# Three page buffers instead of two for the paged FoX sample attention of a two-layer hybrid decoder step

## The reference

```python
k_past = cache_fox_k[l, page_table].reshape(DB, past_len, FOX_H, HEAD_DIM)
v_past = cache_fox_v[l, page_table].reshape(DB, past_len, FOX_H, HEAD_DIM)
...
s_past = jnp.einsum('bthd,bshd->bhts', q, k_past) * scale + (cn[..., :, None] - cp[..., None, :])
s_new = jnp.einsum('bthd,bshd->bhts', q, k) * scale + (cn[..., :, None] - cn[..., None, :])
p = jax.nn.softmax(jnp.concatenate([s_past, s_new], -1), axis=-1)
out = einsum('bhts,bshd->bthd', p[..., :P], v_past) + einsum('bhts,bshd->bthd', p[..., P:], v)
```

## Time and profile before

| | |
|---|---|
| median of 3 runs | 4450.54 us (4433.85 to 4451.39) |
| profiled execution | 4439.32 us, span 4437.8 us |
| PE busy | 4107.8 us, 93% of the span |
| DVE, ACT, POOL busy | 31%, 15%, 7% |
| mean granted TensorE clock | 0.951 |
| DMA | 249.98 MB, mean 56 GB/s |

### The profile page before, as it was taken

One profiled execution on the slowest core, in us unless ns is written; L12 is line 12 of the kernel. 1 busy time (PEld: TensorE's weight loads), 2 busy tenths in 40 slices (PEclk: granted clock), 3 DMA queues, 4 the chain that ended last, 5 costly groups with the idle time before them and its releaser, 6 DMA issues.

```text
span 4437.8 us, 58111 instructions
## 1 busy us (share of the span) xinstructions
PE 4107.8 (93%) x21754; PEld 3067.6 (69%) x21754; DVE 1383.9 (31%) x2997; ACT 664.5 (15%) x1307; POOL 294.6 (7%) x518
## 2 busy tenths in 40 slices
PE   8888999988799999999997889999878899999998
PEld 5677668765457888866656776777545588888665
DVE  3344322334224333300043442233442333332000
ACT  2222101243100000000022221013431000000000
POOL 1000000220200000000010000003111000000000
PEclk9998999999899999999998899999988899999998
DMA  4300020121821111121123001101236111112112
GB/s 125 25 0 0 15 58 25 51 66 58 286 76 29 47 38 45 44 79 39 34 77 10 0 0 36 47 20 47 97 116 221 50 38 47 38 47 84 39 33 64
DMA packets 277954, 249.98 MB, mean 56 GB/s; under 512 B 24636, under 2 KB 237696, under 8 KB 276496
## 3 DMA queue, kind: packets, MB, share of 16 engines
q1 hardware_dynamic: 244400, 144.89, 13.1%
q0 software_dynamic: 33376, 102.70, 7.0%
HBM read 214.70 MB, written 32.83 MB: 56 GB/s over the span
## 4 chain that ended last, share of the span: by engine, by line
PE 82%; DVE 7%; issue 6%; POOLq 2%; POOL 1%; ACT 1%; DMA 1%; DVEq 0%; ACTq 0%; SPq 0%
PE ps L849 78%; PE ps L853 4%; POOL big L749 1%; POOLq L748 1%; POOLq L749 1%; DVE hT L2285 0%; DVE hT L1668 0%; DVE big L1890 0%; ACT wd L2629 0%; DMA ring<-in_w_out 0%; DVE big L1898 0%; DMA big<-in_cache_fox_k 0%; DVE big L1860 0%; DVE big L1853 0%; DVE big L1851 0%
## 5 line engine op out<-in xcount | busy, mean ns | idle before, releaser
L849 PE MATMUL ps<-hT,ring 128*128 128x352 f32 (+1 forms) x3712 | 1073.7, 440 | 23.6 <-DMA ring<-in_w_out 13.2
L849 PEld LDWEIGHTS ps<-hT,ring 128*128 128x128 f32 x3712 | 712.7, 194 | 331.4 <-issue 26.4
L849 PE MATMUL ps<-big,wd 128*128 128x352 f32 (+3 forms) x2576 | 700.2, 431 | 9.7 <-DVE big L1860 7.2
L849 PEld LDWEIGHTS ps<-big,wd 128*128 128x128 f32 (+2 forms) x2576 | 455.1, 189 | 250.5 <-issue 16.1
L849 PE MATMUL ps<-xT,ring 128*128 128x264 f32 x1408 | 345.9, 389 | 13.4 <-DVE xT L2313 13.4
L849 PEld LDWEIGHTS ps<-xT,ring 128*128 128x128 f32 x1408 | 269.5, 192 | 60.7 <-DVE xT L2313 14.2
L849 PEld LDWEIGHTS ps<-ring,hT 128*128 128x128 f32 (+1 forms) x2304 | 259.9, 183 | 16.1 <-issue 13.5
L849 PE MATMUL ps<-ring,hT 128*128 128x128 f32 (+1 forms) x2304 | 265.1, 275 | 2.6 <-ACT xT L2508 2.6
L849 PE MATMUL ps<-hT,wd 128*128 128x264 f32 x1056 | 258.4, 388 | 0.0
L849 PE MATMUL ps<-big 128*128 128x128 f32 (+5 forms) x1492 | 219.0, 308 | 23.6 <-DVE big L1862 7.7
L849 PEld LDWEIGHTS ps<-hT,wd 128*128 128x128 f32 x1056 | 202.2, 191 | 35.2
(11 more groups left out here) (376 smaller groups left out, 3843.3 us busy)
## 6 DMA issues: line engine op xcount, KB each, us to landing
ring<-in_w_in SPq DMA_DIRECT2D x60, 512.0 KB, 3.8
ring<-in_w_gate SPq DMA_DIRECT2D x44, 512.0 KB, 4.1
ring<-in_w_up SPq DMA_DIRECT2D x44, 512.0 KB, 4.1
wd<-in_w_down SPq DMA_DIRECT2D x16, 1408.0 KB, 7.0
x_kept<-xT POOLq DMA_DIRECT2D x32, 528.0 KB, 3.9
xT<-x_kept POOLq DMA_DIRECT2D x32, 528.0 KB, 9.2
big<-in_cache_fox_k SPq DMA_DIRECT2D x64, 256.0 KB, 5.2
big<-in_cache_fox_k POOLq DMA_DIRECT2D x64, 256.0 KB, 5.4
```

The source lines that it names most:

```text
L849: return pe.matmul(out, lhsT, rhs, start=start, stop=stop, skip_group_check=True)
```

## The change

Halves are numbered n = 0 to 7 in the order in which they are used: keys, keys, values, values of group 0, then of group 1. Half n goes into buffer n modulo 3. The third buffer is `fqk` (`xT`): sequence b's pages lie in tiles b and 4 + b, which pair b of the prompt has finished with. So half 2, the first values of group 0, is loaded during the prompt, four pages after each pair. Half 3 waits for `T33`, half 4 for `T73`, half 5 for `V0`, half 6 for `V1` (all of group 0), half 7 for `T33` of group 1. The turned keys of odd units move from the ring to tiles 6 and 7 of `hT`, and `smn` (4 numbers) to the end of tile 4. Behind half 7 SP issues three `w_out` blocks at once, and the fourth, in the slot of `vn`, after `V0` of group 1. POOL waits for `T73` of group 1 before it fetches x back into `xT`. PE's loop over the two groups is written out; those of DVE and ACT stay.

```diff
-        page_at = lambda a, b, j: pages[a][:, b, FW * j:FW * j + FW]
+        def page_at(n, b, j):
+            if n % 3 == 2:
+                return fqk[:, 4 * (j // 2) + b, FW * (j % 2):FW * (j % 2) + FW]
+            return pages[n % 3][:, b, FW * j:FW * j + FW]
...
-        keyt = [region((sil, 0), 4, HPG * PG), region((ringf, 0), 4, HPG * PG)]
+        keys0 = region((sil, 0), 4, HPG * PG)
+        keyt = lambda u, b: hT[:, 6 + b // 2, 512 * (b % 2):512 * (b % 2) + 512] if u % 2 else keys0[:, b, :]
...
-        smn = hT[:, 5, 0:TS]
+        smn = hT[:, 4, NP:NP + TS]
```

On SP:

```diff
-                half("cache_fox_k", key_in, 0, 0, range(1))
+                half(0, range(1))
+                half(2, range(1))
                 sp.wait_ge(fp_dve, FP_DVE.at(l, "1o"))
...
-                half("cache_fox_k", key_in, 0, 1, range(2))
+                half(1, range(2))
+                half(2, range(1, 2))
+                sp.wait_ge(fp_dve, FP_DVE.at(l, "2o"))
+                sp.sem_inc(passed, 1)
+                half(2, range(2, 3))
                 sp.wait_ge(fp_dve, FP_DVE.at(l, "3o"))
...
+                half(1, range(2, 4))
+                half(2, range(3, 4))
+                for n_, it, done in ((3, 2 * l, "T33"), (4, 2 * l, "T73"), (5, 2 * l, "V0"), (6, 2 * l, "V1"), (7, 2 * l + 1, "T33")):
+                    sp.wait_ge(fgr_pe, G_PE.at(it, done))
+                    sp.sem_inc(passed, 1)
+                    half(n_, range(4))
-                sp.wait_ge(fgr_pe, G_PE.at(l * 2 + 1, "F"))
                 for j in range(J_OUT, J_OUT + RING):
+                    if j == J_OUT + RING - 1:
+                        sp.wait_ge(fgr_pe, G_PE.at(l * 2 + 1, "V0"))
                     sp.sem_inc(passed, 1)
                     free(l, j)
                     load(l, j, w_block(l, I["w_out"], P * (j - J_OUT)))
```

On POOL the halves move in the same way (with the odd pages), the third buffer's pages among the prompt's pairs, and x waits:

```diff
+                    if p < 3:
+                        half(2, range(p, p + 1))
...
+                pool.wait_ge(fgr_pe, G_PE.at(2 * l + 1, "T73"))
                 pool.wait_ge(x_out, l * (32 * KT) + 16 * KT)
```

On PE:

```diff
-                with pe.Fori(0, 2) as g:
+                for g in range(2):
...
-                                last = tr(ps[:, 3 + b, P * j:P * j + P], page_at(a, b, j)[:, P * p:P * p + P])
+                                last = tr(ps[:, 3 + b, P * j:P * j + P], page_at(4 * g + a, b, j)[:, P * p:P * p + P])
...
-                                last = mm(ps[o, 7, :], pts[:, HPG * a + j, o], page_at(a, b, j), False, a == 1 and j == HPG - 1)
+                                last = mm(ps[o, 7, :], pts[:, HPG * a + j, o], page_at(4 * g + 2 + a, b, j), False, a == 1 and j == HPG - 1)
```

More of the change, by code:

```diff
@@ L558, in _, with half @@
                 sp.sem_inc(passed, 1)
-                def half(kind, done, g, a, seqs):
+                def half(n_, seqs):
+                    g, a, keys = n_ // 4, n_ % 2, n_ % 4 < 2
+                    kind, done = ("cache_fox_k", key_in) if keys else ("cache_fox_v", value_in)
                     for b in seqs:
@@ L563, in half @@
                             n = sp.value_load(ptab[0:1, bass.ds(g * (4 * NPG) + (b * NPG + a * HPG + j), 1)], min_val=0, max_val=N_POOL - 1)
-                            sp.dma_start(page_at(a, b, j), I[kind][bass.ds(l, 1), bass.ds(n, 1)].rearrange("a n p h d -> p (a n h d)")).then_inc(done[a][0], 16)
-                half("cache_fox_k", key_in, 0, 0, range(1, 4))
+                            sp.dma_start(page_at(n_, b, j), I[kind][bass.ds(l, 1), bass.ds(n, 1)].rearrange("a n p h d -> p (a n h d)")).then_inc(done[a][0], 16)
+                half(0, range(1, 4))
                 sp.wait_ge(fp_dve, FP_DVE.at(l, "0o"))
                 sp.sem_inc(passed, 1)
-                half("cache_fox_k", key_in, 0, 0, range(1))
+                half(0, range(1))
+                half(2, range(1))
                 sp.wait_ge(fp_dve, FP_DVE.at(l, "1o"))
@@ L769, in half @@
                             n = pool.value_load(ptab[0:1, bass.ds(g * (4 * NPG) + (b * NPG + a * HPG + j), 1)], min_val=0, max_val=N_POOL - 1)
-                            pool.dma_start(page_at(a, b, j), I[kind][bass.ds(l, 1), bass.ds(n, 1)].rearrange("a n p h d -> p (a n h d)")).then_inc(done[a][1], 16)
+                            pool.dma_start(page_at(n_, b, j), I[kind][bass.ds(l, 1), bass.ds(n, 1)].rearrange("a n p h d -> p (a n h d)")).then_inc(done[a][1], 16)
                 pool.wait_ge(fg_act, FG_ACT.at(l, "kos"))
@@ L798, in _ @@
                 pool.sem_inc(passed, 1)
[L799 to L810, removed]
+                half(1, range(2, 4))
+                half(2, range(3, 4))
+                for n_, it, done in ((3, 2 * l, "T33"), (4, 2 * l, "T73"), (5, 2 * l, "V0"), (6, 2 * l, "V1"), (7, 2 * l + 1, "T33")):
+                    pool.wait_ge(fgr_pe, G_PE.at(it, done))
+                    pool.sem_inc(passed, 1)
+                    half(n_, range(4))
+                pool.wait_ge(fgr_pe, G_PE.at(2 * l + 1, "T73"))
                 pool.wait_ge(x_out, l * (32 * KT) + 16 * KT)
@@ L1533, in key_scores @@
                         for b in range(4):
-                            last = mm(ps[NS * b:NS * b + NS, a, :], cur_q[:, b, p, :], keyt[u % 2][:, b, :], False, p == 3)
+                            last = mm(ps[NS * b:NS * b + NS, a, :], cur_q[:, b, p, :], keyt(u, b), False, p == 3)
                         G_PE.mark(last, fgr_pe, f"S{u}")
@@ L2220, in _ @@
                             on(gp(f"T{u}{b}"))
-                            gm(v.tensor_copy(keyt[u % 2][:, b, :], ps[:, 3 + b, :]), f"kt{u}{b}")
+                            gm(v.tensor_copy(keyt(u, b), ps[:, 3 + b, :]), f"kt{u}{b}")
                     on(gp(f"S{UNITS[-1]}"))
@@ L2661, in _ @@
                             on(gp(f"T{u}{b}"))
-                            gm(a.copy(keyt[u % 2][:, b, :], ps[:, 3 + b, :]), f"kt{u}{b}")
+                            gm(a.copy(keyt(u, b), ps[:, 3 + b, :]), f"kt{u}{b}")
                     on(gd("neg"))
```

## The result

| | before | after |
|---|---|---|
| median | 4435.33 us of 5 runs (4427.22 to 4451.39) | 4401.91 us of 5 runs (4395.92 to 4406.84) |
| profiled execution, span | 4437.8 us | 4400.2 us |
| mean granted TensorE clock | 0.951 | 0.954 |

The ratio is 0.9916, 95% interval 0.9898 to 0.9933: faster by more than 0.5%. The sign and the mechanism were as forecast; the time, 4401.9, lies 22 us under the 4423.7 and 2 us under the low end of the range. The medians stand 33.4 us apart where the sum said 26.9.

A forecast was written before the change was run, and what follows sets the result against it. PE, 82% of the chain, bounds the kernel; only its transfer waits can go. 11.2 + 12.5 + 0.9 + 0.9 + 1.7 − 0.3 = 26.9 us off the median 4450.5 gives 4423.7 us, range 4404 to 4438.

The forecast's parts named there:

- The sign and the mechanism: Whole kernel: faster, chance 0.68, because PE's waits for keys, values and `w_out` beside the sample attention go.
- the base: Starting time from which the gain was subtracted: the median of the runs, 4450.5 us.
- the clock's two terms: Faster clock once waits go: 0.9 us in group 1's first transposes, 1.7 us in the first eight output matmuls.
- the keys: Sample attention, group 1: half 4 lands early, so PE's key waits of 6.54 and 4.67 us go, 11.2 us.
- the weights: Start of the output jobs: `w_out` issued behind half 7 is hidden, saving 6.29 + 6.17 = 12.5 us.
- the values: Sample attention, group 0 of layer 1: the wait for the second value half goes, 0.9 us.
- What is late next: Half 5, keys of group 1 in the third buffer: there by 1151.4, needed at 1156.9, margin 5.5 us.
- rival 2: Group 1, unit 4: the wait moves to half 5; chance 0.12, or 0.03 for slower than before, such as 4457 us.
- The prompt: Prompt pairs: half 2's loads stretch a store at pair 1's head, costing 0.3 us in all, 1.4 at most.
- Rivals 3 and 4: 3: `w_out` lands no earlier, 4437.8 us, chance 0.10. 4: prompt pays some 15 us at pair heads, 4438, chance 0.05.
- Rival 1: Group 1's transposes and the first output matmuls both run at the high clock: 31.8 us less, 4418.7 us, chance 0.10.

The follow-up runs named there:

- 1: The kernel before, unchanged, run again against itself (the repeated kernel before): 4436.73 us, ratio 1.0002.
- 5: The kernel before with only PE's loop over the two groups written out: 4437.28 us, ratio 0.9995.
- 7: The kernel before with POOL's eight RWKV shift-state stores per layer moved behind its copies for chunk 1: 4437.53 us, ratio 0.9995.
- weights alone (3): The kernel before, two page buffers kept, with turned keys in `hT` and three `w_out` blocks issued behind the last value half: 4430.5 us, ratio 0.9982.
- pages alone (4): The change with the wait for `F` put back ahead of the `w_out` blocks: 4418.16 us, ratio 0.9952.
- 2: The change, unedited, run again against the kernel before (the repeated change): 4405.39 us, ratio 0.9923.
- 6: The change with POOL's eight RWKV shift-state stores per layer moved behind its copies for chunk 1: 4407.08 us, ratio 0.9928.
- 8: The change with POOL's eight RWKV shift-state stores per layer moved behind its copies for chunk 4: 4402.31 us, ratio 0.9924.
- 9: The change without the seven stores per layer of the samples' RWKV shift state: 4393.5 us, ratio 0.9908.

## Why the prediction was right and wrong

The stage of the sample attention, both layers together, in all eleven profiles, each worked out as above, and how much of it PE was busy:

| kernel | stage, us | PE busy in it, us |
|---|---|---|
| before (four: as read, 1, 5, 7) | 249.1, 251.9, 252.5, 251.9 | 181.4, 185.1, 184.2, 183.4 |
| weights alone (3) | 244.4 | 181.8 |
| pages alone (4) | 231.4 | 179.9 |
| the change (five: as read, 2, 6, 8, 9) | 219.9, 219.9, 220.6, 218.0, 220.8 | 176.0, 176.0, 177.1, 174.2, 177.1 |

The windows of the pair as read (columns as in the earlier trace rows), before and after:

```profile
1082.55:1206.46 123.91, 89.64 (x643) 51.48 (x643) 40.29 (x79) 25.30 (x44) 32.62 (x60) 0.78 0.78 273
3268.79:3393.96 125.17, 91.73 (x643) 51.97 (x644) 40.29 (x79) 25.30 (x44) 32.64 (x60) 0.80 0.77 270
```
```profile
1079.54:1190.05 110.51, 88.47 (x643) 50.42 (x643) 40.45 (x79) 25.30 (x44) 28.91 (x54) 0.83 0.78 278
3245.18:3354.54 109.36, 87.51 (x643) 49.69 (x644) 40.45 (x79) 25.30 (x44) 28.90 (x54) 0.83 0.79 281
```

The means of the first and the last line, 251.3 and 219.8, are **31.5 us** apart, and the medians of experiments 1 and 2 stand 31.3 apart. So no part of the gain has to be sought outside this stage. Of the 31.5, PE's idle time gives 24.0 and its busy time 7.4 (rounded): the same number of matmuls runs in less time, at a granted clock of 0.83 over the stage after 0.78 and 0.80.

**What failed, in short.** The forecast of 4423.7 missed by 21.8 us. Of these 13.8 are the base, a median of three runs; 4.4 are the gain, 31.3 instead of 26.9, where the clock's two terms, 0.9 + 1.7 = 2.6, were mis-sized and the runs show 7.4; the last 3.5 are the five runs of the result, whose median lies below that of the six of experiment 2.

**Right:** *the keys, the weights, the values.* All three waits are gone; of `w_out` 0.62 us a layer remain where 0.38 was left over by the sum. The 24.0 us of idle time answer to the 24.6 of these three terms. *What is late next:* nothing; half 5 was in time, and rival 2 fell in both layers, also in its slower form. *The prompt:* pairs 1 to 3, from the end of pair 0 to that of pair 3, took 138.93 us before and 140.68 after in layer 0, 137.99 and 136.27 in layer 1: no cost that shows, where −0.3 was taken. By the Trainium skill, "DMA: Bandwidth & Descriptors", section "Issuing engines are not separate DMA queues", 1.4 us would have been lost; these rows, −1.75 and +1.72, show no such loss in the sum of the two layers. But the same stretch of layer 0 took 142.27 in the repeated kernel before, 3.3 us more than in the first, so a loss of this size could hide. Rivals 3 and 4 fell too.

**Wrong, the base:** "from the median the time is **4423.7**". The three runs had their median at 4450.5; 24 runs beside experiments 1 and 2 gave 4436.7, so 13.8 us of the miss are in the start and none of them in the change. Single runs follow the granted clock of the whole execution: of the 24, the two at 0.946 took 4449.1 and 4456.0 us, the one at 0.955 took 4423.5. The profiled execution at hand, 4439.3, was nearer, and the sum against it, 4412.4, would have been 7 us off the 4405.4 of the repeated change. The low end, 4404, was set between the two places that the fastest of three runs gave; it had to hold a low base and a larger gain together.

**Wrong, the clock:** "I take the middle, **1.7**" for the first output matmuls. They took 4.05 + 4.49 before and 2.60 + 2.60 after, a gain of 3.3, near the upper end of 3.5; over all profiles their mean fell from 9.1 to 5.2. The windows of the change (PE, PEld, DVE, ACT, POOL busy, granted clock, DMA share, GB/s) show the two places where I set rows against each other:

```profile
1137.80:1140.50 2.70, 2.63 (x7) 1.36 (x7) 0.01 (x1) 0.00 (x0) 0.99 (x3) 0.77 1.02 354
1140.40:1147.00 6.60, 6.60 (x45) 6.41 (x49) 2.14 (x4) 2.26 (x4) 2.89 (x6) 0.57 1.03 396
...
1187.60:1190.20 2.60, 2.59 (x9) 1.75 (x10) 0.00 (x0) 0.00 (x0) 0.00 (x0) 1.00 0.00 0
```

Behind 0.62 us of idle time the output jobs start and stay at 1.00 (2.4 GHz). Behind 1.57 us the decay matmuls get 0.77, and the transposes after them 0.57, close to 1.2 GHz, with PE busy throughout; in layer 1 the two are 0.80 and 0.75. So the row of the decay matmuls was no neighbour of the output jobs, and the row at 1.00 was. The transposes gained 0.3 (11.56 to 11.29) where 0.9 was taken; over all profiles they gained 1.6 (means 12.2 and 10.6). The other 1.9 us of the 7.4 lie in matmuls of the stage for which the sum had no term. That gap length decides is argued from these two places only: behind the same 1.57 us the transposes took 4.82 to 6.42 us in the five profiles of the change. Rival 1, for which both places run high, was right for one and wrong for the other. The Trainium skill, "TensorE: Matmul & The Clock Gate", section "What's actually happening", by which the sum was 31.7 (31.4 with the prompt's −0.3, which it leaves out), agrees with the total of 31.5 but not with the row at 0.57, where PE had work and ran throttled.

**Wrong, one execution for all:** the profile I read had the shortest stage of four, 249.1 against 251.9 to 252.5. Its waits were as long as the others': keys took 11.2, 12.3, 12.6 and 13.9 us in the four, `w_out` 13.2, 11.6, 11.6 and 12.5, and PE's idle time was 67.7 there and 67.8 in the mean of the other three. Its busy time was 181.4 against 184.2. So the clock makes the difference here too, between the 29.2 of the first pair and 31.5.

**What the parts are worth.** By the table, pages alone give 251.3 − 231.4 = 19.9 us, weights alone 6.9; together 31.5, or 4.7 more than the sum. Each removes the other's traffic: without early pages the weights leave late and beside x; without early weights the pages' gain is followed by a wait that slows the clock. That is the reading of two profiles, one of each part. The prediction priced the two as independent, and came out near only because it took the weights' leaving with the early pages in place.

**Open.** What PE waits for at the first RWKV chunk is not named by the profile; that it is program code behind a slow block is my reading of the instruction queue, and no run tells it from another request on the same engines. Nor is it known what ACT and DVE wait for when the stores are issued later, or why the clock of a chunk is 0.83 at one time and 0.96 at another.

## What to carry to other kernels

Before setting a forecast on a median of three, look how far single runs lie apart, and forecast the difference on the base that the most executions agree on. A wait that is removed also gives back the clock behind it: price that by whether an idle gap stays, and how long it is against gaps in the same trace that did and didn't cost the clock; and count all the work behind the wait, not its first matmuls alone. Two parts of a change that use the same transfers are to be priced together.

## What the runs showed of the hardware that was not expected

Seven stores of 4 KB each in 4-byte elements, issued in 6 us, kept the DMA engines occupied long after. Their issue in layer 0, then the windows 175 to 200 us of the change, and of the same without those stores (columns as above):

```profile
161.31 6.19 POOL L682 DMA_DIRECT2D out_rwkv_shift_sample<-shift_rows_out  x7
```
```profile
175.00:200.00 25.00, 19.05 (x136) 16.34 (x137) 11.59 (x25) 7.69 (x18) 0.99 (x2) 0.86 1.04 22
```
```profile
175.00:200.00 25.00, 20.34 (x152) 17.45 (x152) 11.95 (x26) 7.51 (x16) 0.99 (x2) 0.86 0.00 1
```

A share of 1.04 at 22 GB/s beside a share of 0.00: without the stores the projection block was through before this stretch begins. In the sample attention a share of 1.03 moved 396 GB/s. Yet the medians of the whole program stand only 9 to 12 us apart, and not clear of the noise: in the same windows PE was busy for 19.05 of the 25 us with the stores and for 20.34 without them.

Chunks of the same work ran at 0.83 or at 0.96 within one layer (experiment 9), with no difference in the kernel that would say which. Executions of one program follow suit: the 24 of the kernel before lie between 4423.5 and 4456.0 us, by and large the longer the lower their granted clock.
